# Eight forgetting-gate columns projected by token beside the recurrence's values, then turned

## The reference, cut to what matters

```python
h = _rmsnorm(x, pre_norm_g[l])
proj = jnp.einsum('btd,de->bte', h, w_in[l])
q_a, f_a, i_a, g_a, u_b, g_b, q_c, k_c, v_c, g_c, f_c = jnp.split(proj, IN_SPLIT_POINTS, axis=-1)
...
log_f_c = jax.nn.log_sigmoid((f_c + fox_f_bias[l]).astype(jnp.float32))
...
c = jnp.cumsum(log_f, axis=1).transpose(0, 2, 1)      # in the forgetting attention
bias = jnp.where(mask, c[:, :, q0:q1, None] - c[:, :, None, :q1], 0.0)
```

## Time and profile before

| | us |
|---|---|
| median of 3 runs | 1584.03 (1581.96 to 1585.93) |
| the profiled execution, its own time | 1581.26 |
| its span in the profile | 1579.5 |
| PE busy, share of the span | 1532.5 (97%) |
| DVE busy | 894.6 (57%) |
| ACT busy | 695.7 (44%) |
| 16 DMA engines, q1 | 23.1% |

### The profile page before, as it was taken

One profiled execution on the slowest core, in us unless ns is written; L12 is line 12 of the kernel. 1 busy time (PEld: TensorE's weight loads), 2 busy tenths in 40 slices (PEclk: granted clock), 3 DMA queues, 4 the chain that ended last, 5 costly groups with the idle time before them and its releaser, 6 DMA issues.

```text
span 1579.5 us, 33484 instructions
## 1 busy us (share of the span) xinstructions
PE 1532.5 (97%) x14426; PEld 1266.6 (80%) x14426; DVE 894.6 (57%) x1651; ACT 695.7 (44%) x1268; POOL 120.6 (8%) x86
## 2 busy tenths in 40 slices
PE   7999999899999999999999999999999999999998
PEld 6787867779789797897887677888887888888887
DVE  3658364656474574842245998433246677777323
ACT  5543264563352633524234998423235333333222
POOL 0004000002230322302000000000000000000000
PEclk9999989999999999999999999999999999999999
DMA  6322212431020110206312000223332323323231
GB/s 222 108 81 81 93 41 100 158 107 37 16 68 11 54 36 17 67 11 149 80 54 80 2 2 2 94 83 104 107 134 93 107 81 107 105 83 107 77 121 70
DMA packets 110978, 124.40 MB, mean 79 GB/s; under 512 B 21320, under 2 KB 94664, under 8 KB 110448
## 3 DMA queue, kind: packets, MB, share of 16 engines
q1 hardware_dynamic: 107904, 114.85, 23.1%
q10 hardware_dynamic: 2928, 7.41, 1.4%
HBM read 118.04 MB, written 4.21 MB: 77 GB/s over the span
## 4 chain that ended last, share of the span: by engine, by line
PE 84%; DVE 9%; ACT 5%; issue 2%; POOL 0%; DMA 0%; DVEq 0%; SPq 0%; ACTq 0%; POOLq 0%
PE bank L807 80%; PE bank L817 4%; ACT arena L1487 3%; DVE arena L2098 2%; DVE arena L2095 2%; DVE weights_lo L2095 1%; ACT L1487 1%; DVE arena L2102 1%; ACT weights_hi L1487 1%; DVE arena L2270 1%; DVE arena L2462 0%; DVE extra L2095 0%; DVE arena L2188 0%; DMA arena<-in_x 0%; ACT extra L1487 0%
## 5 line engine op out<-in xcount | busy, mean ns | idle before, releaser
L1487 ACT ACTIVATE arena<-bank 128x512 f32<-128x512 f32 (+3 forms) x415 | 225.3, 569 | 554.4 <-PE bank L807 528.0
L2095 DVE TENSOR_TENSOR weights_lo<-weights,weights_hi 128x1024 fp32r<-128x1024 f32 (+1 forms) x190 | 239.3, 1260 | 304.6 <-ACT weights_hi L1487 297.4
L807 PE MATMUL bank<-h_hi,weights_hi 128*128 128x512 f32 (+1 forms) x1008 | 400.8, 398 | 4.1 <-DVE h_lo L2098 1.9
L807 PE MATMUL bank<-h_lo,weights_hi 128*128 128x512 f32 (+1 forms) x1008 | 393.9, 391 | 0.0
L807 PE MATMUL bank<-h_hi,weights_lo 128*128 128x512 f32 (+1 forms) x1008 | 393.9, 391 | 0.0
L807 PE MATMUL bank<-arena 64*64 64x64 f32 (+6 forms) x7746 | 344.0, 247 | 14.7 <-DVE arena L2098 5.9
L807 PEld LDWEIGHTS bank<-arena 64*64 64x64 f32 (+3 forms) x7746 | 281.0, 140 | 68.2 <-issue 57.2
L1487 ACT ACTIVATE weights_hi<-weights 128x1024 fp32r<-128x1024 f32 (+1 forms) x190 | 200.1, 1053 | 172.3 <-PE bank L807 169.5
L807 PEld LDWEIGHTS bank<-h_hi,weights_hi 128*128 128x128 f32 (+1 forms) x1008 | 189.9, 188 | 50.8 <-issue 6.9
L807 PEld LDWEIGHTS bank<-h_hi,weights_lo 128*128 128x128 f32 (+1 forms) x1008 | 189.9, 188 | 40.6
L807 PEld LDWEIGHTS bank<-h_lo,weights_hi 128*128 128x128 f32 (+1 forms) x1008 | 190.0, 188 | 37.5
(11 more groups left out here) (172 smaller groups left out, 1628.2 us busy)
## 6 DMA issues: line engine op xcount, KB each, us to landing
weights<-in_w_in SPq DMA_DIRECT2D x39, 1024.0 KB, 5.3
weights<-in_ffn_up SPq DMA_DIRECT2D x22, 1024.0 KB, 5.1
weights<-in_ffn_down SPq DMA_DIRECT2D x10, 1024.0 KB, 5.0
weights<-in_w_out SPq DMA_DIRECT2D x8, 1024.0 KB, 5.0
weights<-in_w_in SPq DMA_DIRECT2D x16, 256.0 KB, 4.4
weights<-in_w_branch_rwkv SPq DMA_DIRECT2D x4, 1024.0 KB, 5.2
weights<-in_w_branch_nsa SPq DMA_DIRECT2D x4, 1024.0 KB, 5.2
weights<-in_w_in SPq DMA_DIRECT2D x5, 512.0 KB, 3.7
```

The costliest lines, as they stand in the source:

```text
L807: return pe.matmul(o, w, x, start=first, stop=last)
L1487: return act.activation(o, i, f, **kw)
L2095: return dve.tensor_tensor(o, a, b, op)
```

## The change: what it does

`fc0` is gone from the list. The use of `i` gets a second source: 8 columns from column 3584 on, behind its 256, so its rows are 264 wide, its matmuls move 264 columns, and slots and pieces grow from 2048 and 1024 to 2112 and 1056 elements. ACT copies 8 columns of each of the four token tiles to `fc_tok`. After the keys, PE multiplies them by the identity in four matmuls into a new job `fc` (8 rows by 512 tokens), and ACT adds the bias from there. The absolute value follows in DVE's part of `i`, exp and ln in ACT's part of `gc0` (now apart from those of `hg_log`), the log sigmoid and the running sum behind `level_sub(2)` in DVE's part of `gc1`. SP's wait for `fox_decay`, with the write and the broadcast load, moves from ahead of the use of `gc2` to ahead of the use of `qc0`. The first use is now that of `f0` and `f1`.

```diff
-SLOT = 2048
-PIECE = 1024
+SLOT = 2112
+PIECE = 1056
...
-P1 = ("fc0", "f0", "f1", "q0", "q1", "ga0", "ga1", "gb0", "gb1", "i", "gc0", "gc1", "gc2", "gc3",
+P1 = ("f0", "f1", "q0", "q1", "ga0", "ga1", "gb0", "gb1", "i", "gc0", "gc1", "gc2", "gc3",
...
+        fc_tok = view(2560, TT, FOX_HEADS, of=extra)
...
                 jobs("hk", 2)
+                jobs("fc", 1)
...
-        channels(base["p1", "fc0"], (0, cols(w1, 3592 - 104, 3592)))
...
-        tokens(base["p1", "i"], w1, 512, 256)
+        tokens(base["p1", "i"], w1, None, 256 + FOX_HEADS, runs=((0, 512, 256), (256, 3584, FOX_HEADS)))
...
-                if n == use_of[base["p1", "gc2"]]:
+                if n == use_of[base["p1", "qc0"]]:
                     sp.wait_ge(sem("fox_decay"), 1)
...
-                    to_tokens(base["p1", name], h_both, 256)
+                    to_tokens(base["p1", name], h_both, 256 + FOX_HEADS)
                     pe.wait_ge(sem("hg_scaled"), 2)
                     for n in range(2):
                         transposes(base["hk"] + n, [hg_k[:, n, c * P:(c + 1) * P] for c in range(TT)])
+                    for i in range(TT):
+                        wait_read(pe, base["p1", "i"] + i)
+                    claim(pe, base["fc"])
+                    for i in range(TT):
+                        ins = mm(ps(base["fc"])[0:FOX_HEADS, i * P:(i + 1) * P], fc_tok[:, i, :], ident)
+                    fill(base["fc"], ins)
...
                 elif kind == "i":
                     for i in range(TT):
-                        copy_out(j + i, hv_tok[:, i, :], width=256)
+                        wait_full(act, j + i)
+                        run(hv_tok[:, i, :], ps(j + i)[:, 0:256], ACT.Copy)
+                        read(j + i, run(fc_tok[:, i, :], ps(j + i)[:, 256:256 + FOX_HEADS], ACT.Copy))
...
                 if name == "q1":
-                    act.wait_ge(sem("fox_abs"), 1)
-                    m = mark(run(fc_e[0:8, :], fc_abs[0:8, :], ACT.Exp, scale=-1.0))
                     act.wait_ge(sem("hg_abs"), 1)
                     m = mark(run(hg_log, hg_log, ACT.Exp, scale=-1.0))
                     act.wait_ge(act_step, m)
-                    run(fc_e[0:8, :], fc_e[0:8, :], ACT.Ln, bias=1.0).then_inc(sem("fox_log"), 1)
                     run(hg_log, hg_log, ACT.Ln, bias=1.0).then_inc(sem("hg_logs"), 1)
...
                 elif name == "i":
                     for n in range(2):
                         copy_out(base["hk"] + n, hk_tok[:, n, :])
+                    wait_full(act, base["fc"])
+                    read(base["fc"], run(fc_x[0:8, :], ps(base["fc"])[0:8, :], ACT.Identity, bias=params("fox_bias")[0:8]))
+                elif name == "gc0":
+                    act.wait_ge(sem("fox_abs"), 1)
+                    m = mark(run(fc_e[0:8, :], fc_abs[0:8, :], ACT.Exp, scale=-1.0))
+                    act.wait_ge(act_step, m)
+                    run(fc_e[0:8, :], fc_e[0:8, :], ACT.Ln, bias=1.0).then_inc(sem("fox_log"), 1)
...
                 elif name == "i":
                     tt(hg_k, hg_k, k_a, ALU.mult).then_inc(sem("hg_scaled"), 1)
+                    wait_read(dve, base["fc"])
+                    stt(a8, x8, -1.0, x8, ALU.mult, ALU.max).then_inc(sem("fox_abs"), 1)
...
                     level_sub(LEVEL_AFTER[name] + 1)
+                    if name == "gc1":
+                        dve.wait_ge(sem("fox_log"), 1)
+                        then(stt(l8, x8, 0.0, e8, ALU.min, ALU.subtract))
+                        then(ts(a8, x8, 0.0, 1.0, ALU.mult, ALU.add))
+                        dve.tensor_tensor_scan(n8, a8, l8, 0.0, ALU.mult, ALU.add).then_inc(sem("fox_decay"), 1)
```

More of the change, by code:

```diff
@@ L1590, in _ @@
                 x_root(0, i, norm_1)
-            stream_to(base["p1", "fc0"], 0)
+            stream_to(base["p1", P1[0]], 0)
             have(act, "par")
@@ L1632, in _ @@
                     copy_out(j, k_c[:, n, :])
-                elif kind == "fc":
-                    wait_full(act, j)
-                    read(j, run(fc_x[0:8, :], ps(j)[96:104, :], ACT.Identity, bias=params("fox_bias")[96:104]))
                 else:
@@ L2301, in _ @@
                     read(j, ins)
[L2302 to L2305, removed]
+                if name == "q0":
                     for n in range(2):
@@ L2326, in _ @@
                     level_take(0)
[L2327 to L2331, removed]
                 elif name == "gb1":
@@ L2835, in _layouts @@
     put("pool_scale", by_tile(a["pool_scale"][0]))
-    par[96:104, PCOLS["fox_bias"][0]] = a["fox_f_bias"][0]
+    put("fox_bias", a["fox_f_bias"][0][:, None], FOX_HEADS)
     put("mu_rkv", by_tile(mu[:3072]))
```

## The result

| | before | after |
|---|---|---|
| median us, 22 runs each | 1581.86 (1579.46 to 1585.93) | 1585.24 (1581.81 to 1589.63) |
| ratio to before | | 1.0021, 95% interval 1.0014 to 1.0028 |
| span of the profiled execution | 1579.5 | 1582.0 |

A forecast was written before the change was run, and what follows sets the result against it. PE, with 84% of the chain, was taken to bound the kernel, with the start waiting for data. Terms -5.44 + 1.45 - 2.73 + 0.32 + 0.85 + 0.75 = -4.8 us gave 1579.2 us from 1584.03, range 1575.5 to 1584.

The forecast's parts named there:

- first projection starts: At the start: the first use, now 1024 KB instead of 416, lands later and delays PE's first projection, +1.45 us.
- idle time ahead of `i`: PE's 2.73 us wait for `weights_lo` goes, as ACT's exp and ln leave `q1` and DVE's steps leave `gb0`: -2.73.
- `i`, 96 matmuls of 264 columns: In `i`: 8 more columns in each of 96 matmuls cost 0.0033 us each, +0.32 us, bounds 0 and +0.6.
- four matmuls that turn: Behind the keys' transposes: four fp32 matmuls moving 128 columns at 0.21 us each, +0.85 us, bounds 0.44 and 1.25.
- waits at `gc2`, `gc3`: PE waits for `weights_lo` after ACT's table loads and DVE's moved decay steps; +0.75 us counted for the stage.
- everything behind it: All that follows the start of `u0` was to lie 4.8 us earlier, to the end of the kernel.
- 3% longer on ACT and DVE, hidden: In `i`: its pieces take ACT and DVE 3% longer, at no cost in time.
- the projection in the slow stretch: `fc0` goes, but the slow clock then falls on `f0`, so the gain is one projection at full clock: -5.44 us.
- D: Rival, 0.08: from `gc1` on, new ACT and DVE work reaches PE in series; +2.3, 1586.3 us, or 1590.4 with dearer switches.
- C: Rival, 0.18: nothing given back; start costs +0.5, turning 0.44, ACT's new work hides; -6.9, 1577.1 us.
- A: Rival, 0.14: table switches ahead of `gc2`'s piece cost more than their row, PE waits 3.4 us; -2.1, 1581.9 us.
- B: Rival, 0.10: start transfers run later, the piece of `f1` comes at 26.4, PE stands 1.8 us; -3.0, 1581.0 us.

The follow-up runs named there:

- e1: Changed kernel, but second half of the `weights_hi` ring 1088 elements behind the first instead of 1056: 1575.01 us, 0.9956 to the kernel before.
- e2: Kernel before, with only the second half of `weights_hi` 1056 elements behind the first instead of 1024: 1589.71 us, ratio 1.0049.
- e6: Kernel before, with both halves of `weights_hi` 128 bytes higher, still 4096 bytes apart: 1604.96 us, ratio 1.0138.
- e7: Kernel before, with the second half of `weights_hi` 1040 elements (4160 bytes) behind the first: 1591.78 us, one run.
- e5: Kernel before, with arena and both weight rings 128 bytes higher, distances within unchanged: 1581.78 us, ratio 0.9995.
- e10: Kernel before, with the raw ring alone (`weights_lo`) 128 bytes higher modulo 256, `weights_hi` 256 bytes further: 1593.19 us, ratio 1.0064.
- e9: Kernel before, with both weight rings 128 bytes higher while `h` and all else PE reads stay: 1603.52 us, ratio 1.0121.
- e8: Changed kernel, step 1088, gates' exp and ln ahead of `gc0`'s sigmoid, decay steps in `gc0`, first use cut into `f0` and `f1`: 1573.38 us, 0.9937.

## Why the prediction was wrong

Its steps, each against the trace of the changed kernel:

| step | forecast | measured |
|---|---|---|
| first projection starts | 17.9 | 17.93 |
| the first use's landing, as ACT sees it | 12.9 | 12.84 |
| idle time ahead of `i` | 0 | 0 |
| `i`, 96 matmuls of 264 columns | 12.1 (+0.32) | 11.65 (+0.03) |
| four matmuls that turn | 0.85 | 0.97 |
| waits at `gc2`, `gc3` | 0.7, 0.5 | 0.52, 0.33 |
| ACT waits for the use of `qc0` | none | none |
| `u0` starts | 104.9 | 105.17 |
| everything behind it | 4.8 earlier | from 4.5 earlier to 2.5 later |

What was reckoned locally came out near the forecast; the last line did not, and the cause was no term at all. The step that failed is the sentence that the pieces of `i` are "3% longer on ACT and DVE, hidden": it took the growth of slots and pieces as a matter of how long they are, for the engines that write them, and did not ask where they then lie, for the engine that reads them. That growth is in the diff's first lines and holds for all 189 pieces of the kernel, not for the two of `i`. It put the second half of `weights_hi` 4224 bytes behind the first, which costs 6.7 ns in each matmul with 512 moving columns that uses it. e1 gives the missing term: 10.2 us by the medians (1585.24 and 1575.01), and e2 finds 7.7 in the old kernel with nothing else changed; the intervals of the two overlap. With this term left out, e1's 0.9956 (-7.0 us, interval -9.2 to -4.7) takes in the forecast -4.8 at its edge; the gain at 137 us was 5.5.

Some of the close hits are luck. In e1, without the slow pieces, `u0` starts at 104.24, 5.5 us earlier than before. In the changed kernel these pieces had already cost 0.9 by then, and that brought it to 105.17, near the 104.9 forecast. One term better than forecast was the projection in the slow stretch: `f0` took 6.18 us in e1 (17.84 to 24.02) where `fc0` took 6.66. The term of `i` was mis-sized: start to start it took 11.62 us before (70.86 to 82.48) and 11.65 after. The 11.77 of the earlier trace rows is a stretch of the chain, measured otherwise. The term of the four turning matmuls came near with a wrong price: the trace has eight records for them, 0.11 us apart, not four of 0.21.

Of the rivals none was this one. D, the only one that ended slower, wanted 5.5 us of idle time between `gc1` and `u0`; there are 0.85. C's -6.9 lies near e1's -7.0 by luck, since its terms did not come true. A fell: a table switch costs its 1.28 us, the exp starts 1.29 behind the start of the load, so the drain that the Trainium skill adds (ScalarE: Activation LUTs, What ACT_TABLE_LOAD costs) does not show in these rows. B is out by the absence of a wait at `f1`, C by the first projection's start at 17.93 and the 0.97 us of the turning. The test named for the prediction, that everything behind `u0` would lie 4.8 earlier, was the one that caught it.

## What to carry to other kernels

When a change moves a buffer or alters a stride, reckon what it does to every reader for the whole run, before the terms of the stage in which it was made: a shift of 6.7 ns in a distance of 226.7 is 3%, and a lead of 5 us is eaten by it in some 60 projections (half of them slow, 0.16 us each) where PE alone sets the pace. In kernels like this one, keep the tiles that TensorE loads and those that it streams at one offset modulo 256 bytes (0 was free here, 64 and 128 were not, others were not tried), and give a ring a step of its own, not the size of its largest piece. To find such a loss, compare the distance of one kind of instruction in code that both kernels share; busy shares (97% in both) and waits do not show it.

## What the runs showed of the hardware

- fp32r matmuls with 512 moving columns, each with its own load of 128 x 128: 226.7 ns apart when both operands' tiles have the same place modulo 256 bytes, 233.3 when the weights' tiles are 128 bytes off (e6), and 653 and 652 matmuls in 150 us, in place of 664, when every second piece is 128 or 64 bytes off (e2, e7). Moving everything together changes nothing (e5). A distance grows when the running matmul's weights or the next one's are off (e6, e10); with both weights off the mean is a little under that of `weights_hi` alone (232.4, e9). Why the place matters stays open.
- The cost is smaller where the weights are streamed and the other operand is loaded, in `ffn_down`: e6 has distances of 232, 228 and 226 ns there (from 1477 us on), all three 226 to 227 before. The matmuls of `i`, with 256 moving columns, do not show it: their median distance is 120 ns before and in e6.
- Growing the moving columns from 256 to 264 lengthened the 96 matmuls of `i` little: 11.65 us beside 11.62, of which the old ones lost some 0.1 on starting behind idle time (0.22 from the first to the second, 0.12 between later ones). That leaves about 1.4 ns each, where 3.3 were forecast.
- Idle time of 0.82 us ahead of the last transposes left the granted clock at 1.00 from 16 to 18 us (e8), 2.58 us did not: 0.51 (the changed kernel). The later stretches at the low clock differed from profile to profile: 0.83 from 200 to 230 us before, 0.89 in the changed kernel and e1, and from 260 to 300 us 0.91 in e1 and 1.00 in the other two. Leads behind 200 us wander with them by one or two microseconds.
